# First norm tiles of a hybrid decoder block: one half of the norm weights by DMA, two of the four first transposes and one stripe in another order

## The reference

```python
def rmsnorm(x, g):
    xf = x.astype(jnp.float32)
    y = xf * lax.rsqrt(jnp.mean(xf * xf, axis=-1, keepdims=True) + EPS)
    return (y * g.astype(jnp.float32)).astype(x.dtype)

h = rmsnorm(x, g_mix[i])          # x: 1024 x 1024, g_mix: 1024 weights
z = h @ w_in[i]                   # w_in: 1024 x 1536
a = z[..., :C_CONV]
b = z[..., C_CONV:2 * C_CONV]
v = z[..., 2 * C_CONV:]
u = a * jax.nn.sigmoid(b)
u = causal_depthwise_conv(u, conv_w[i], conv_b[i])
...
x = x + mix @ w_out[i]            # then FFN, per-layer input, final rmsnorm
```

## Time and profile before

| | us |
|---|---|
| median of 3 runs | 1008.56 (1008.40 to 1008.79) |
| the profiled execution, whole | 1009.25 |
| its span, from first to last instruction | 1007.4 |
| PE busy in the span | 994.6 |
| first product of data (`first_part(0, front)`) starts | 14.98 |

### The profile page before, as it was taken

One profiled execution on the slowest core, in us unless ns is written; L12 is line 12 of the kernel. 1 busy time (PEld: TensorE's weight loads), 2 busy tenths in 40 slices (PEclk: granted clock), 3 DMA queues, 4 the chain that ended last, 5 costly groups with the idle time before them and its releaser, 6 DMA issues. The chain is left out here.

```text
span 1007.4 us, 12472 instructions
## 1 busy us (share of the span) xinstructions
PE 994.6 (99%) x4543; PEld 825.0 (82%) x4543; DVE 754.1 (75%) x1013; ACT 464.8 (46%) x713; POOL 385.8 (38%) x284
## 2 busy tenths in 40 slices
PE   8999999999999999999999999999999999999996
PEld 7888888888888888888888888888888888888785
DVE  5899999956699665665765764763677888885997
ACT  6724438504363333333333333333445665575764
POOL 3356797810146354354354454451000000011754
PEclk9999999999999999999999999999999999999998
DMA  7421102552213333332432432413998797533222
GB/s 254 137 84 42 66 19 104 210 167 84 105 55 101 118 105 87 123 105 76 133 105 73 136 105 65 145 64 108 353 379 307 236 312 256 190 103 105 85 101 87
DMA packets 103375, 138.25 MB, mean 137 GB/s; under 512 B 6107, under 2 KB 60915, under 8 KB 103315
## 3 DMA queue, kind: packets, MB, share of 16 engines
q1 hardware_dynamic: 103170, 137.21, 40.8%
q10 hardware_dynamic: 144, 0.26, 0.1%
HBM read 104.68 MB, written 32.77 MB: 136 GB/s over the span
## 5 line engine op out<-in xcount | busy, mean ns | idle before, releaser
L698 POOL TENSOR_SCALAR ss<-ss 128x1 f32<-128x1 f32 x38 | 17.7, 466 | 324.6 <-ACT junk L960 302.3
L2018 DVE SCALAR_TENSOR_TENSOR ps<-resid,convw,ps 128x512 f32<-128x512 f32 x190 | 127.4, 747 | 0.0
L1533 PE MATMUL ps<-ring_hi,ring_lo 128*128 128x512 f32 x308 | 120.0, 390 | 0.1
L1535 PE MATMUL ps<-ring_hi 128*128 128x512 f32 x308 | 119.8, 389 | 0.0
L1534 PE MATMUL ps<-ring_lo,ring_hi 128*128 128x512 f32 x308 | 119.8, 389 | 0.0
L1533 PE MATMUL ps<-act_hi,bs_lo 128*128 128x512 f32 x240 | 93.6, 390 | 0.0
L1535 PE MATMUL ps<-act_hi,bs_hi 128*128 128x512 f32 x240 | 93.4, 389 | 0.0
L1534 PE MATMUL ps<-act_lo,bs_hi 128*128 128x512 f32 x240 | 93.4, 389 | 0.0
L946 ACT ACTIVATE ring_hi<-raw 128x512 fp32r<-128x512 f32 x89 | 51.9, 625 | 60.4 <-PE ps L1535 60.4
L704 POOL TENSOR_TENSOR wc_lo<-raw_b,wc_hi 128x1024 fp32r<-128x1024 f32 x22 | 58.9, 2676 | 47.9 <-ACT wc_hi L946 46.7
L1931 DVE TENSOR_TENSOR ring_lo<-raw,ring_hi 128x512 fp32r<-128x512 f32 x89 | 58.0, 688 | 22.4 <-ACT ring_hi L946 22.3
(11 more groups left out here) (271 smaller groups left out, 2721.8 us busy)
## 6 DMA issues: line engine op xcount, KB each, us to landing
raw<-in_w_gate_up SPq DMA_DIRECT2D x44, 512.0 KB, 5.2
raw<-in_scratch SPq DMA_DIRECT2D x52, 256.0 KB, 3.4
raw<-in_w_down SPq DMA_DIRECT2D x52, 256.0 KB, 4.0
in_scratch<-in_s SPq DMA_DIRECT2D x44, 256.0 KB, 2.9
in_scratch<-gtmp SPq DMA_DIRECT2D x33, 256.0 KB, 2.3
keep<-in_w_down SPq DMA_DIRECT2D x32, 256.0 KB, 4.2
keep<-in_scratch SPq DMA_DIRECT2D x25, 256.0 KB, 3.6
resid<-in_x SPq DMA_DIRECT2D x8, 512.0 KB, 8.7
```

Source lines behind the costliest of these rows:

```text
L698: pool.tensor_scalar(ss[:, n:n + 1], ss[:, n:n + 1], 1.0 / D, EPS, ALU.mult, ALU.add)\
L1533: pe.matmul(dst, w_lo_, m_hi, start=start, stop=False, skip_group_check=onto)
L1535: return pe.matmul(dst, w_hi_, m_hi, start=False, stop=stop, skip_group_check=onto)
L2018: dve.scalar_tensor_tensor(out=conv_c if k == last_odd else acc, in0=u_all[:, c, k + h * BANK:k + (h + 1) * BANK], scalar=convw[:, c * 32 ...
```

## The change

One half of the norm weights (the upper 512) is no longer spread by PE, but by a DMA that reads the same 2 KB for each of the 128 partitions, into the SBUF tile `gain`. The DMA stands in SP's list behind the load of tile 1 and ahead of stripe 0. The lower half still goes through PE. So `normed` takes its weights from PSUM for the lower half and from `gain` for the upper one, as two instructions of 512 for each of the tiles 0 to 4 (before: two for tile 0, one of 1024 for tiles 1 to 4), and its first instruction now waits for the DMA. ACT later copies only the lower half from PSUM to `gain`. PE has one spreading product less and two identity products less (11 instead of 13), one of them now between `turn(0)` and `turn(1)`. On ACT, tile 0's high part comes ahead of stripe 0's. POOL makes stripe 0's low part in two halves with a semaphore each. On PE, `turn(3)` comes ahead of the second half of `first_part(1, front)`, and on ACT its high part ahead of `square_x(5)`.

```diff
             load_x(0, xres[:, 0, :])
-            sp.dma_start(raw_b[0:1, 0, :], g_mix).then_inc(gain_in, DMA)
+            sp.dma_start(raw_b[0:1, 0, 0:BANK], g_mix[:, 0:BANK]).then_inc(gain_in, DMA)
             load_x(1, xres[:, 1, :])
+            sp.dma_start(gain[:, BANK:D], g_mix[0, BANK:D].partition_broadcast(P)).then_inc(spread_in, DMA)
             load_stripe(0, 0, first_in)
...
             norm_1(1)
-            split_cols(0, 1)
+            pool.wait_ge(w_hi, 1)
+            lo(cols_stripe(ws_lo, 0)[:, 0:4, :], cols_of(raw, 0)[:, 0:4, :], cols_stripe(ws_hi, 0)[:, 0:4, :], w0_half)
+            lo(cols_stripe(ws_lo, 0)[:, 4:8, :], cols_of(raw, 0)[:, 4:8, :], cols_stripe(ws_hi, 0)[:, 4:8, :], w_lo)
...
             square_x(1)
+            turned_hi(0, 0)
             split_cols(0, DMA, signal=first_in)
-            turned_hi(0, 0)
             turned_hi(1, 0)
...
             turned_hi(2, 0)
+            turned_hi(3, 0)
             square_x(5)
-            turned_hi(3, 0)
             act.wait_ge(xn_ok, 5)
-            copy(gain[:, :], pair(2), gain_ok)
+            copy(gain[:, 0:BANK], ps[:, 2, :], gain_ok)
...
             pe.wait_ge(gain_in, DMA)
-            for d in range(2):
-                last = pe.matmul(ps[:, 2 + d, :], raw_b[0:1, 1, 0:P], raw_b[0:1, 0, d * BANK:(d + 1) * BANK],
-                                 start=True, stop=True)
-                last.then_inc(gain_ok, 1)
-            keep_warm(4)
+            pe.matmul(ps[:, 2, :], raw_b[0:1, 1, 0:P], raw_b[0:1, 0, 0:BANK], start=True, stop=True).then_inc(gain_ok, 1)
+            keep_warm(3)
             turn(0, 0)
+            keep_warm(1)
             turn(1, 0)
-            keep_warm(4)
+            keep_warm(2)
...
+            pe.wait_ge(w0_half, 1)
+            pe.wait_ge(act_lo_ok, 4)
+            first_part(0, front, range(4))
             pe.wait_ge(w_lo, 1)
-            pe.wait_ge(act_lo_ok, 4)
-            first_part(0, front)
+            first_part(0, front, range(4, KD))
             pe.wait_ge(w_lo, 2)
             first_part(1, front, range(4))
             turn(2, 0)
+            turn(3, 0)
             first_part(1, front, range(4, KD))
-            turn(3, 0)
             turn(4, 0)
...
                 if n == 0:
                     dve.wait_ge(gain_ok, 1)
+                    dve.wait_ge(spread_in, DMA)
...
-                for c in (slice(0, BANK), slice(BANK, D)) if n == 0 else (slice(0, D),):
-                    if n == 0 and c.start:
-                        dve.wait_ge(gain_ok, 2)
+                for c in (slice(0, BANK), slice(BANK, D)) if n < 5 else (slice(0, D),):
                     ins = dve.scalar_tensor_tensor(out=xn_place(n)[:, c], in0=x_tile(t, norm)[:, c], scalar=rs[:, n:n + 1],
-                                                   in1=pair(2)[:, c] if n < 5 else gain[:, c],
+                                                   in1=ps[:, 2, :] if n < 5 and c.start == 0 else gain[:, c],
                                                    op0=ALU.mult, op1=ALU.mult)
```

More of the change, by code:

```diff
@@ L175, in hybrid_block @@
         e_in = [sem(f"e_in{j}") for j in range(3)]
-        gfin_in = sem("gfin_in")
+        spread_in = sem("spread_in")
         out_stored = [sem(f"out_stored{j}") for j in range(2)]
@@ L179, in hybrid_block @@
         tables_ok = sem("tables_ok")
-        upad_ok = sem("upad_ok")
+        w0_half = sem("w0_half")
         ss_ok = sem("ss_ok")
@@ L294, in hybrid_block @@
         N_IN, N_PLE, N_WO = 12, KP, KD
-        N_TABLES = 2 + sum(2 << g for g in range(GROUPS))
+        N_TABLES = 3 + sum(2 << g for g in range(GROUPS))
         GU0 = N_IN + N_PLE + N_WO
@@ L670, in _ @@
             load_e(0)
-            sp.dma_start(raw_b[:, 0, :], g_ple_post[0].partition_broadcast(P)).then_inc(gfin_in, DMA)
+            sp.dma_start(raw_b[:, 0, :], g_ple_post[0].partition_broadcast(P)).then_inc(spread_in, DMA)
             load_e(1)
-            sp.dma_start(raw_b[:, 1, :], g_final.partition_broadcast(P)).then_inc(gfin_in, DMA)
+            sp.dma_start(raw_b[:, 1, :], g_final.partition_broadcast(P)).then_inc(spread_in, DMA)
             load_e(2)
@@ L731, in _ @@
             pool.wait_ge(xn_ok, 4)
-            pool.memset(u_all[:, :, 0:PAD], 0.0).then_inc(upad_ok, 1)
+            pool.memset(u_all[:, :, 0:PAD], 0.0).then_inc(tables_ok, 1)
             for g in range(GROUPS):
@@ L899, in times_post @@
                 if t == 0:
-                    pool.wait_ge(gfin_in, 2 * DMA)
+                    pool.wait_ge(spread_in, 3 * DMA)
                 e = e_place(t)
@@ L977, in evac_ab @@
                 if n == 0:
-                    act.wait_ge(upad_ok, 1)
+                    act.wait_ge(tables_ok, 2)
                 if n >= 2:
@@ L1502, in _ @@
             act.wait_ge(fs4_ok, FS + m + 1)
-            act.wait_ge(gfin_in, 2 * DMA)
+            act.wait_ge(spread_in, 3 * DMA)
             copy(pair(2), raw_b[:, 1, :], gain_ok)
@@ L1631, in _ @@
             pe.wait_ge(const_in, 6 * DMA)
-            pe.wait_ge(gain_ok, 3)
+            pe.wait_ge(gain_ok, 2)
             for c in range(KC):
@@ L1944, in normed @@
                     dve.wait_ge(gain_ok, 1)
+                    dve.wait_ge(spread_in, DMA)
                 elif n == 5:
-                    dve.wait_ge(gain_ok, 3)
+                    dve.wait_ge(gain_ok, 2)
                 elif t == 0:
@@ L2389, in final @@
                 if t == 0:
-                    dve.wait_ge(gfin_in, 2 * DMA)
+                    dve.wait_ge(spread_in, 3 * DMA)
                 x_ = x_tile(t, 3)[:, c]
@@ L2439, in _ @@
             dve.wait_ge(res_ok, t + 1)
-            dve.wait_ge(gain_ok, 4)
+            dve.wait_ge(gain_ok, 3)
             dve.tensor_tensor(raw[:, 2, C0], x_tile(t, 3)[:, C1], pair(2)[:, C1], ALU.mult).then_inc(xg_ok, 1)
```

## The result

| | before | after |
|---|---|---|
| median of 12 runs, us | 1008.68 (1008.40 to 1009.39) | 1010.69 (1009.90 to 1012.51) |
| ratio, 95% interval | | 1.0021 (1.0012 to 1.0030) |
| profiled execution, whole | 1009.25 | 1010.40 |
| its span | 1007.4 | 1008.3 |
| first product of data starts | 14.98 | 15.78 |

The changed kernel is 2.0 us slower, where the sum had 0.33 faster; it lies 2.5 us above the predicted 1008.2 and 0.8 above the range. A repeat gave 1011.08 beside 1008.76 (1.0024, 1.0015 to 1.0032). The times of the changed kernel also spread more: over 2.6 us against 1.0.

A forecast was written before the change was run, and what follows sets the result against it. PE was taken to bound the kernel, nearly without a gap from the first product at 14.98 us. First product 0.47 earlier, 0.14 lost at PE's second wait: -0.33 us, giving 1008.2 from the median, range 1007.4 to 1009.9.

The forecast's parts named there:

- the sum: First product 0.47 earlier plus 0.14 lost later: -0.33 us; as a check, net is the spread's landing less 7.63.
- What bounds the kernel: PE, busy 994.6 of 1007.4 us, runs nearly without a gap from the first product; nothing behind has slack.
- the second wait: PE's wait of 0.58 us at 24.28 for DVE's `act_lo`; tile 4's longer norm was to lose 0.14 there.
- the list of signs: What would show it: DVE start 7.3, transposes near 8.8 and 11.0, first product near 14.5, PE's second wait 0.7.
- The landing of the spread: DVE's first instruction waits for the spread DMA: taken at 7.3 us, between ends of 7.1 and 8.75.
- late spread: At DVE's first instruction: spread lands at 8.75 behind a late tile 1, +1.1 us, 1009.7; chance 0.24.
- out on both sides: The profiled execution's 0.69 us above the median was left out both before and after the change.
- hidden, with 0.05 to spare: ACT's stripe 0 high part between tiles 0 and 1 costs nothing; with faster PE, up to 0.5 on the path.
- the last start: PE's start after standing still; a clock rise 5.9 us later comes at 14.7 and costs 0.1.
- Nothing changes: An earlier clock shortens transposes, which then wait for ACT's stripe; the gain is eaten, 1008.6; chance 0.14.
- The late clock: The gap ahead of the first product delays the clock's rise; products at half speed, up to +3.0, 1009.7; chance 0.12.
- My 0.04 for slower by over 0.2%: Chance given to a measurable slowdown (0.2%, 2.0 us); faster had 0.02, same 0.94.

The follow-up runs named there:

- the repeat: The kernel before run again with no edit: 1008.59 beside 1008.88 (0.9997, 0.9988 to 1.0006).
- PE is kept busy: Nine identity products instead of three in the changed kernel: 1011.20 beside 1008.76 (1.0023); with ACT's stripe 0 order also undone, 1009.95 beside 1008.89 (1.0011).

## Why the prediction was wrong

**What bounds the kernel: right.** From the first product to the one behind the second wait it was 9.39 us after and 9.30 before, and nothing behind took up the shift. The loss there was forecast at 0.14 and measured 0.09, but not in the wait: that was 0.54 and not the 0.7 of the list of signs, and PE took 0.13 longer to reach it. Tile 3's new place gave 0.04 (9.26 in the kernel with it alone), next to nothing, as said.

**The landing of the spread: the step that failed first.** I took 7.3 from a range of 7.1 to 8.75; DVE began at 8.71, past the 7.6 that was to show the forecast wrong, and at 8.8 to 9.1 in four other profiles and 10.0 in a fifth with the spread at this place. The form of the sum held: net is the landing less 7.63, so +1.0 with 8.66 put in, and the two profiled spans differ by 0.9. The first product would be at 15.87 by that form and was at 15.78. So the mechanism of the "late spread" rival is what happened, with another cause. I had put it on tile 1's lag, which did not recur (6.1 instead of 8.06), and waved at the repeated reads with 0.2 us. The runs put most of it on these: with other rows as the source the landing was 1.0 us earlier in the pair of profiles, and the time 1.2 to 1.6 less in the medians. The other 0.4 of the 1.36 us between 7.3 and 8.66 came with distinct rows too. My price of "0.26 MB at the 377 GB/s of that slice" was one of bytes at full rate, from transfers that each read their own rows.

**The base: the second step that failed.** I left the profiled execution's 0.69 above the median "out on both sides". It was not the same on both sides. It came from a late clock, and only by some 0.1 us from the late tile 1, and a usual execution of before has its first product near 14.0 to 14.6 (14.02 in the repeat, 14.26 to 14.64 in the three kernels with the halves or tile 3's place alone or together). With the clock up, ACT gets tile 1's banks sooner; the new order forbids it to use that.

**ACT's order: "hidden, with 0.05 to spare".** True only of that one execution, with its late clock. I wrote that up to 0.5 would be on the path with a faster PE, and 0.4 from the stripe in one piece. Where PE is kept busy the runs say 0.9 from DVE's start to the first product (6.85 against 5.94) and 1.25 in the medians; alone in the kernel before, with the stripe in one piece, 1.2. In the changed kernel it costs nothing beyond PE's standstill, and the standstill nothing beyond it.

**The clock.** As forecast, it did not reach the first products: they are 0.12 apart from 15.78 on. But the 5.9 us from "the last start" to the rise had no ground. I counted from 7.78, and the earlier trace rows show PE at work without a gap from 4.07 to there; and in the changed kernel the rise came behind the transposes in one profile and within those of tile 1 in the other, with the same standstill ahead.

**Outside the span.** 0.25 us that no step of mine looked at.

**The account.** The 2.0 us between the medians are 1.15 between the two profiled executions (0.9 in the span, 0.25 outside), 0.57 by which the profiled one of before lies above its median, and 0.29 by which that of the changed kernel lies below its own. The 0.9 is the landing and the 0.57 the base; what makes the last, a usual execution of the changed kernel later than its profiled one, no trace shows for certain. The profile at 1011.69 with ACT's order undone had tile 1 at 8.1 and the spread at 10.0, so later landings are one candidate.

**The rivals.** "Nothing changes" named the right mechanism (an early clock, and ACT's stripe in its way) and priced it as the end of a gain, not as a loss on top of a late spread. I gave each rival alone a time; two of them held at once. The late clock was shown in one profile, of the kernel with the spread first. It would fit the changed kernel's runs at 1012.3 to 1013.1, which no profile shows, but so would a landing later still. My 0.04 for slower by over 0.2% was too small: the ratios of 1.0021 and 1.0024 lie just past it, though both intervals reach below it.

## What to carry to other kernels

A DMA that reads the same small piece for every partition should not be priced by its bytes alone, least of all where a whole chain of engines waits for it; look for a row of the same kind at a quiet time, or try other rows as its source. Before costing an edit at nothing with a few hundredths of margin, ask which execution the margin is from: here it held for the profiled one and not for the usual ones. And where two causes cover each other, undoing one shows nothing; undo both, and measure from the event that starts the chain to the one that ends it, which takes the scatter of the start out.

## What the runs showed of the hardware

- 128 reads of the same 2 KB landed 1.0 us later than 128 reads of different 2 KB rows of another tensor, at the same place in the queue (8.7 against 7.7). The engines moved 162 and 138 GB/s in the two slices in question, and 128 and 211 with the different rows.
- The clock rose at very different times in executions of like kernels: within the first transposes (16 in 2.53 us), at their end (3.83 us), or only near 19 us, after PE had stood still twice. The profile prints 1.00 as granted for these first stretches all the same; only the durations tell the level (transposes of 424 against 272 to 275 ns, products of 416 against 281).
- PE stood still for 1.35 and 0.65 us in the kernel with the spread first, and its products ran at the lower level up to 19 us. The Trainium skill (TensorE: Matmul & The Clock Gate, What's actually happening) has it that activity releases the throttle. This one profile agrees.
- The time outside the span goes with the program (medians): 1.85 to 1.90 us in the kernel before and the four others that have stripe 0 in one piece, 2.11 to 2.19 in the nine that have it in halves.
